# Down projection of the gated feed-forward by seven half-block products over pairs of inner tiles

## What is computed

```python
def conv_ffn(h, w_up, conv_w, conv_b, w_down):
    u = h @ w_up                       # 1024 -> 2 * 2816
    u = depthwise_conv(u, conv_w, width=3) + conv_b
    g, val = jnp.split(u, 2, axis=-1)
    return (jax.nn.silu(g) * val) @ w_down     # 2816 -> 1024
x = x + conv_ffn(rmsnorm(x, ffn_norm_g[i]), ...)
```

## Time and profile before

| | us |
|---|---|
| median of three runs | 2869.74 |
| lowest, highest | 2862.95, 2871.09 |
| profiled execution | 2867.41 |
| its span, first to last instruction | 2865.6 |
| PE busy in the span | 2743.9 |
| DVE, POOL, ACT busy | 1777.1, 1455.1, 1356.6 |

### The profile page before, as it was taken

How to read it: one execution, slowest core, us unless ns; L and a number is a source line. 1 busy time by engine, 2 the same in 40 slices (tenths; PEclk the granted TensorE clock), 3 DMA queues, 4 the chain that set the end, 5 groups by cost and what they waited for, 6 DMA issues and landing times. The chain is left out here.

```text
span 2865.6 us, 40261 instructions
## 1 busy us (share of the span) xinstructions
PE 2743.9 (96%) x13708; PEld 2308.6 (81%) x13708; DVE 1777.1 (62%) x2481; ACT 1356.6 (47%) x2102; POOL 1455.1 (51%) x1119
## 2 busy tenths in 40 slices
PE   8899999999989999999989999998898999999998
PEld 6788888877878888788878888887787788887886
DVE  6577777773654455555478887887527445545555
ACT  5577777763444444311256665665414444443212
POOL 2355555442587777543553333332226877774443
PEclk9999999999999999999999999999899999999999
DMA  3000000003122122522020010000320212225221
GB/s 137 23 11 10 7 7 10 15 1 149 57 89 88 67 87 88 198 99 106 15 112 23 32 35 24 30 26 13 151 105 30 103 73 88 88 72 221 88 88 59
DMA packets 54395, 195.37 MB, mean 68 GB/s; under 512 B 6544, under 2 KB 9872, under 8 KB 53776
## 3 DMA queue, kind: packets, MB, share of 16 engines
q1 hardware_dynamic: 54288, 193.95, 18.6%
HBM read 148.84 MB, written 45.09 MB: 68 GB/s over the span
## 5 line engine op out<-in xcount | busy, mean ns | idle before, releaser
L1209 PE MATMUL ffn_ps<-ffn_b_hi,weights_hi 128*128 128x512 f32 x704 | 278.6, 396 | 19.1 <-POOL weights_lo L720 10.2
L1210 PE MATMUL ffn_ps<-ffn_b_lo,weights_hi 128*128 128x512 f32 x704 | 276.6, 393 | 0.0
L1211 PE MATMUL ffn_ps<-ffn_b_hi,weights_lo 128*128 128x512 f32 x704 | 276.6, 393 | 0.0
L360 POOL TENSOR_TENSOR weights_lo<-weights_raw,weights_hi 128x1024 fp32r<-128x1024 f32 (+2 forms) x65 | 127.0, 1960 | 215.6 <-ACT weights_hi L355 215.6
L1100 POOL TENSOR_TENSOR ffn_y_lo<-ffn_y_raw,ffn_y_hi 128x1024 fp32r<-128x1024 f32 x44 | 109.0, 2498 | 231.1 <-ACT ffn_y_hi L1030 231.1
L720 POOL TENSOR_TENSOR up_local_lo<-up_sums,up_local_hi 128x512 fp32r<-128x512 f32 x126 | 171.4, 1363 | 96.8 <-ACT up_local_hi L715 96.8
L2301 ACT ACTIVATE dif_p<-dif_s,dif_neg_max 128x1024 f32<-128x1024 f32 x128 | 142.2, 1114 | 124.5 <-DVE dif_neg_max L2488 116.5
L1209 PE MATMUL ffn_ps<-ffn_b_hi,up_local_hi 128*128 128x512 f32 x504 | 196.3, 390 | 0.0
L1210 PE MATMUL ffn_ps<-ffn_b_lo,up_local_hi 128*128 128x512 f32 x504 | 196.1, 389 | 0.0
L1211 PE MATMUL ffn_ps<-ffn_b_hi,up_local_lo 128*128 128x512 f32 x504 | 196.1, 389 | 0.0
L1030 ACT ACTIVATE ffn_y_hi<-ffn_y_raw 128x1024 fp32r<-128x1024 f32 x44 | 44.2, 1051 | 315.0 <-PE ffn_ps L1211 315.0
(11 more groups left out here) (353 smaller groups left out, 8530.3 us busy)
## 6 DMA issues: line engine op xcount, KB each, us to landing
weights_raw<-in_up SPq DMA_DIRECT2D x44, 512.0 KB, 3.8
up_raw<-in_up SPq DMA_DIRECT2D x44, 512.0 KB, 4.1
ffn_products<-ffn_conv SPq DMA_DIRECT2D x44, 512.0 KB, 2.7
ffn_y_raw<-ffn_products SPq DMA_DIRECT2D x44, 512.0 KB, 4.1
ffn_down_raw<-in_down SPq DMA_DIRECT2D x24, 512.0 KB, 6.3
weights_raw<-in_diff_qkv SPq DMA_DIRECT2D x23, 512.0 KB, 3.6
weights_raw<-in_down SPq DMA_DIRECT2D x20, 512.0 KB, 5.9
x_spill<-x_in SPq DMA_DIRECT2D x16, 512.0 KB, 3.9
```

Source lines behind the costliest of these rows:

```text
L360: pool.tensor_tensor(w.lo[:], w.raw[:], w.hi[:].bitcast(F32), ALU.subtract).then_inc(w.lo_done, 1)
L1209: pe.matmul(out, hi, x_hi, start=start, stop=False, skip_group_check=True)
L1210: pe.matmul(out, hi, x_lo, start=False, stop=False, skip_group_check=True)
L1211: return pe.matmul(out, lo, x_hi, start=False, stop=stop, skip_group_check=True)
```

## The change

The down projection takes the same seven products as the up projection, over *pairs of inner tiles*. The weights of a pair (2 tiles x 8 output tiles) are split in four half blocks: A11 and A21 are the even tile's output tiles 0 to 3 and 4 to 7, A12 and A22 the odd tile's. The pair of y tiles is split in B11, B12 (even tile, left and right positions) and B21, B22 (odd tile). Sums of weights: S1 = A21 + A22, S2 = S1 - A11, S3 = A11 - A21, S4 = A12 - S2. Of y: T1 = B12 - B11, T2 = B22 - T1, T3 = B22 - B12, T4 = B21 - T2.

- **In the up projection** DVE makes T1 behind the gated product of an even tile and T2, T3, T4 behind that of an odd one (`finish_y`). SP stores B11 and T1, or B21, B22, T2, T3 and T4, each of 128 x 512, in place of one 128 x 1024 tile. ScalarE's centre tap of the value waits for those stores.
- **Groups** (`SUPER`): six; the first has one pair, the others two. A group has seven steps (`DOWN_A`, 42 in all). A step is one product: 4 output tiles x 1 or 2 pairs x 3 passes = 12 or 24 matmuls into 4 banks.
- **Order of the queues**: SP's `fetch(g)` loads y block n when step n of the group before is over, or its low part is done (n = 0, 1). The odd weights follow behind step 2. POOL makes the four sums and all low parts of weights in one fixed order. ScalarE's `high` copies a step's weights and then its y block, step by step. DVE makes the low parts of y, four steps ahead (`low_y(step + 4)`, then `add_product(step)`).
- **Additions**: steps 0, 1 of a group go to a buffer `common`, step 3 to `fifth`, the others straight to a quarter of `x_out`. In the last group DVE adds `common` and `fifth` to the quarters (16 additions) before the last three steps' own. Step 2 accumulates on step 0's banks and step 6 on step 5's, so TensorE's step 6 waits until DVE has read step 5's banks (`use = step - 1`); the others wait for the step two or three before.
- The order of the final squares and the place of `sq` follow.

```diff
+DOWN_A = ("A11", "S2", "A12", "S1", "S4", "S3", "A22")
+DOWN_SUMS = ("S1", "S2", "S4", "S3")
+SUPER = [(0, 1)] + [(2 * g - 1, 2) for g in range(1, 6)]
+STEPS = 7 * len(SUPER)
...
+            def fetch(g):
+                for n in range(2):
+                    sp.wait_ge(y_lo_done, 7 * g - 7 + n + 1)
+                    load_y(g, n)
+                sp.wait_ge(a_summed, 4 * g)
+                sp.wait_ge(a_lo_done, 7 * g - 6)
+                load_a(g, 0)
+                multiplied(sp, 7 * g - 5)
+                load_y(g, 2)
+                sp.wait_ge(a_lo_done, 7 * g)
+                load_a(g, 1)
+                for n in range(3, 7):
+                    multiplied(sp, 7 * g - 7 + n)
+                    load_y(g, n)
...
+            def high(g, n):
...
+                multiplied(act, step - 7)
+                if name in DOWN_SUMS:
+                    act.wait_ge(a_summed, 4 * g + DOWN_SUMS.index(name) + 1)
+                else:
+                    act.wait_ge(even_loaded if name == "A11" else odd_loaded, 32 * g + 16)
+                act.activation(down.a_hi[name][:, 0:width], down.a_raw[name][:, 0:width], ACT.Copy).then_inc(a_hi_done, 1)
+                act.wait_ge(y_loaded[n], 16 * g + 16)
+                act.activation(down.b_hi[n][:, 0:width], down.b_raw[n][:, 0:width], ACT.Copy).then_inc(y_hi_done, 1)
...
+            def sum_a(g, name, first, second, op, loads, sums):
...
+                multiplied(pool, 7 * g - 7 + DOWN_A.index(name))
...
+            for g in range(len(SUPER)):
+                sum_a(g, "S1", "A21", "A22", ALU.add, (even_loaded, odd_loaded), 0)
+                sum_a(g, "S2", "S1", "A11", ALU.subtract, (), 1)
+                low_a(g, "A11")
+                sum_a(g, "S4", "A12", "S2", ALU.subtract, (), 2)
+                pool.wait_ge(a_summed, 4 * g + 3)
+                low_a(g, "S2")
+                low_a(g, "A12")
+                low_a(g, "S1")
+                sum_a(g, "S3", "A11", "A21", ALU.subtract, (), 0)
+                low_a(g, "S4")
+                low_a(g, "S3")
+                low_a(g, "A22")
...
+            low_y(0)
+            low_y(1)
             finish(PAIRS - 1, 1)
...
+            add_product(0)
+            finish_y(PAIRS - 1, False)
+            low_y(2)
+            low_y(3)
+            low_y(4)
+            for step in range(1, LAST_COMMON + 1):
+                low_y(step + 4)
+                add_product(step)
...
+            add_common(6)
+            add_common(4)
+            add_product(STEPS - 3)
+            add_common(5)
+            add_product(STEPS - 2)
+            add_product(STEPS - 1)
...
-                        for z in range(2):
-                            mm = passes(bank(DOWN_BANKS[n % NACC]), down_hi[s][z][:, m, :], down_lo[s][z][:, m, :],
-                                        y_hi[s][:, z, cols], y_lo[s][:, z, cols], z == 0, z == 1)
-                        mm.then_inc(acc_ready, 1)
...
+                more = n in (2, 6)
+                use = step - {0: 3, 6: 1}.get(n, 2)
+                for i in range(4):
...
+                        pe.wait_ge(acc_added, added(use, i))
+                    for j in range(width):
+                        mm = passes(bank(DOWN_BANKS[4 * second + i]), down.a_hi[name][:, j, i, :],
+                                    down.a_lo[name][:, j, i, :], down.b_hi[n][:, j, :], down.b_lo[n][:, j, :],
+                                    j == 0 and not more, j == width - 1)
+                    mm.then_inc(acc_ready, 1)
```

More of the change, by code:

```diff
@@ L1040, in _ @@
             act.wait_ge(c21_done, PAIRS - 1)
[L1041 removed]
+            act.wait_ge(y_done, PAIRS - 1)
+            act.wait_ge(y_stored, stored(PAIRS - 1, False))
             centre(1, PAIRS - 1, 1)
[L1044 to L1054 removed]
+            for step in range(2, STEPS):
+                high(step // 7, step % 7)
             if ahead:
@@ L1109, in _ @@
-            groups(pool, step)
+            def sum_a(g, name, first, second, op, loads, sums):
+                width, raw_a = SUPER[g][1], down.a_raw
+                for done in loads:
+                    pool.wait_ge(done, 32 * g + 16 * width - (16 if g else 0))
+                need(pool, a_summed, 4 * g + sums)
+                multiplied(pool, 7 * g - 7 + DOWN_A.index(name))
+                pool.tensor_tensor(raw_a[name][:, 0:width], raw_a[first][:, 0:width], raw_a[second][:, 0:width],
+                                   op).then_inc(a_summed, 1)
@@ new lines, in shared, with add_common @@
+            def shared(n, i):
+                return added(LAST_COMMON, 3) + {6: 4, 4: 8, 5: 16}[n] + i + 1
+            def add_common(n):
+                for i in range(4):
+                    if n != 6:
+                        dve.wait_ge(acc_added, added(LAST_COMMON, 3) + i + 1)
+                    dve.tensor_tensor(x_part(n, i), x_part(n, i), (down.common if n == 6 else down.fifth)[:, i, :],
+                                      ALU.add).then_inc(acc_added, 1)
+            low_y(0)
+            low_y(1)
@@ new lines, in _ @@
+            finish(PAIRS - 1, 1)
+            add_product(0)
[6 more added lines that the diff above has]
+                add_product(step)
+            for i in range(4):
+                dve.wait_ge(acc_added, added(LAST_COMMON, i))
+                dve.tensor_tensor(down.fifth[:, i, :], down.fifth[:, i, :], down.common[:, i, :],
+                                  ALU.add).then_inc(acc_added, 1)
@@ new lines, in _ @@
+            multiply_down(0)
+            fourth(PAIRS - 1)
+            for step in range(1, STEPS):
+                multiply_down(step)
+            parts = ((out_norm.acc, 1, 0, out_norm.sq_added, 12), (out_norm.acc, 0, 0, out_norm.sq_added, 15),
+                     (sq[:, 1, :], 0, HALF, out_norm.sq_ready, 16))
+            for i, (squares, half, place, ready, count) in enumerate(parts):
+                pe.wait_ge(ready, count)
+                for t in range(4 * half, 4 * half + 4):
+                    mm = pe.matmul(out_norm.psum_sum[:, t:t + 1], squares[:, place + t * P:place + (t + 1) * P],
+                                   ones[:, 0:1], start=(i == 0 and t == 4), stop=(i == 2 and t == 3),
+                                   skip_group_check=True)
@@ L1304 @@
+            mm.then_inc(out_norm.sq_summed, 1)
 class Latent:
```

299 lines of the change are left out of this document (180 added, 119 removed).

## The result

The changed kernel took **2951.95 us** (median of four runs, 2947.85 to 2963.81) against 2867.74 us for the kernel before: ratio 1.0302, 95% interval 1.0266 to 1.0337, 3.0% slower. I had forecast 2923 us and a range up to 2946: the sign was right, the size too small by 29 us, and the time lies above the range. The profiled execution took 2963.81 us, with a span of 2961.5; it is the longest of the four, so sums made from its trace are up to 12 us larger than the medians say.

The account below looks back on a forecast made before the run. TensorE's instruction count was taken as the bound. Per layer 212.2 + 27.2 + 20.9 + 3.6 + 6.0 = 269.9 us, + 2.6 behind; both layers add 53.4 to 2867.4, median 2.3 above: 2923 us, range 2885 to 2946.

Parts of the forecast that it names:

- Removed work: Down projection: 924 matmuls a layer remain, 132 fewer, saving 29.9 us a layer, 59.8 us for both, all on the path.
- I take nothing: Up projection: DVE's added subtractions, 0.69 us each, delay block sums by 2.1 us in odd cycles but cost TensorE 0 us.
- gaps in the loop of the up projection: Sign in the up projection's loop: gaps there would show that its three subtractions were misjudged; it should stay 100% busy.
- The fallback of 20 us: Up projection: if the cover is gone, 1 us in 20 cycles is 20 us, half of it kept in the upper end.
- The low clock: Down projection: six new stalls a layer of over 3.5 us, each followed by 1.0 us lost at low clock: 6 us.
- The change of group: Down projection, groups 1 to 4: TensorE's seventh step waits for DVE's additions, 5.2 us each, 20.9 us a layer.
- a split port: Alternative to DVE and POOL taking turns: both run on at a slower rate, a layer's stretch some 10 us shorter.
- The first group: Start of the down projection, one pair with short steps: waits of 1.15, 3.5, 8.4, 2.5 and 11.6, 27.2 us a layer.
- The end: End of the down projection: DVE's shared additions, 0.68 us each, make the last step start 3.6 us late.
- waits feed each other: Rival, both layers: transfers at 6.3 us and more, low clock after each stall; +76 us, 2946; chance 0.17.

## Why the prediction was too low, point by point

- **Removed work.** Right: 924 matmuls a layer. Of the 616 first passes of both layers 528 stand in the rows of after, against the earlier trace rows:

```profile
L1372 PE MATMUL ffn_ps<-ffn_y_hi,ffn_hi_S x352: 389/389/796, 1209.7 to 2923.5; 128*128 128x512 f32 x176
...
L1372 PE MATMUL ffn_ps<-ffn_y_hi,ffn_hi_A x176: 387/389/767, 1202.5 to 2936.6; 128*128 128x512 f32 x176
```

- **The step that failed: "I take nothing" for the up projection.** It measured 15.7 and 15.6 us a layer. I had read from the earlier trace rows that a DVE instruction with both operands in SBUF waits for a POOL instruction to end, and even listed the product at 1174.87 with its 1.78 us, but priced three differences at 0.69 each, from a row whose second operand lies in PSUM. Beside POOL two of them took 1.56 and 1.78 us and the product ahead of them 2.02, the sums come 4.8 us later instead of 2.1, and the 1.21 us of slack in the earlier trace rows and the cycle behind it are used up. The sign that I had named for this, gaps in the loop of the up projection, came. The fallback of 20 us stood in the text for the case that the cover is gone; 31.3 us came in the two layers. I had also written that half of the 20 is kept in the upper end, but the upper end of 2946 is the rival's sum without it. With those 10 us the range would have reached 2956 and held the result, by an allowance and not by the mechanism.
- **The low clock: 6.0 us a layer forecast, 17.7 and 15.3 measured** (what the starts of matmuls without a wait lie further apart than 0.2267 us). I counted six stalls a layer of over 3.5 us at 1 us each; my own list had eight of 3.5 us and more, and ten in all. The trace of after has ten stalls a layer, and shorter ones pulled the clock down too. After 2.75 us idle in layer 0:

```profile
1331.21 0.47 PE L1372 MATMUL ffn_ps<-ffn_y_hi,ffn_hi_A 128*128 128x512 f32 x1 [2.75 <-DVE x_first L1331]
...
1332.67 0.59 PE L1372 MATMUL ffn_ps<-ffn_y_hi,ffn_hi_A 128*128 128x512 f32 x1
1333.06 0.63 PE L1373 MATMUL ffn_ps<-ffn_y_lo,ffn_hi_A 128*128 128x512 f32 x1
...
1336.04 0.44 PE L1374 MATMUL ffn_ps<-ffn_y_hi,ffn_lo_A 128*128 128x512 f32 x1
```

  Eight matmuls 0.43 us apart instead of 0.23. Layer 0's down projection has 81 such matmuls, layer 1's 70; before, seven (I had read eight) and none.
- **The change of group: mechanism right, size too large.** Forecast 4 x 5.2 us; measured 2.65, 2.75, 3.91, 2.83 and 3.33, 2.92, 3.20, 3.09. The rows of DVE and POOL at the second of them, whose group starts at 1295.66:

```profile
1318.62 2.39 POOL L1176 TENSOR_TENSOR ffn_raw_S<-ffn_a_raw 128x1024 f32<-128x1024 f32 x1 [9.86 <-DMA ffn_a_raw<-in_down]
```

```profile
1325.62 1.32 DVE L1306 TENSOR_TENSOR ffn_y_lo<-weights_raw,ffn_y_hi 128x1024 fp32r<-128x1024 f32 x1 [7.32 <-ACT ffn_y_hi L1117]
1326.86 2.47 DVE L1331 TENSOR_TENSOR x_first<-x_first,ffn_ps 128x512 f32<-128x512 f32 x4
1329.25 1.21 DVE L1306 TENSOR_TENSOR ffn_y_lo<-ffn_y_raw,weights_hi 128x1024 fp32r<-128x1024 f32 x1
1330.39 2.47 DVE L1331 TENSOR_TENSOR x_first<-x_first,ffn_ps 128x512 f32<-128x512 f32 x4
```

  POOL's S1 starts 23.0 us into the group (forecast 22.7), the first low part ends at 31.3 (31.2). The second low part was free to go at once, 1.21 us; I had it wait for POOL's sum S4, 3.5 us. Here DVE came first and POOL's next instruction had to wait (3.43 us for 2.4). Which of the two gets its turn first I had taken against DVE. The 10 us that I gave for a split port were not worked out from rows, and no run shows them.
- **The first group: 27.2 us forecast, 23.9 and 25.3 measured.** Its five stalls in layer 0 were 2.74, 3.30, 5.84, 4.06 and 7.91 us, against 1.15, 3.5, 8.4, 2.5 and 11.6.
- **The end: 3.6 us forecast, 12.2 and 5.7 measured.** The same omission as in the up projection. The shared additions have both operands in SBUF, and in layer 0 POOL prepares the next stage's weights and sums squares beside them:

```profile
1449.77 6.89 DVE L1358 TENSOR_TENSOR ffn_fifth<-ffn_fifth,ffn_common 128x512 f32<-128x512 f32 x4
1456.59 4.68 DVE L1342 TENSOR_TENSOR x_first<-x_first,ffn_common 128x512 f32<-128x512 f32 x4
```

```profile
1448.18 5.22 POOL L360 TENSOR_TENSOR weights_lo<-weights_raw,weights_hi 128x1024 fp32r<-128x1024 f32 x2 [10.82 <-ACT weights_hi L355]
...
1454.57 4.95 POOL L1208 TENSOR_TENSOR ffn_sq<-ffn_sq 128x512 f32<-128x512 f32 x3
```

  In layer 1, with POOL idle, four of them take 2.49 us, and only the last four, beside the squares, more:

```profile
2916.53 2.49 DVE L1342 TENSOR_TENSOR x_second<-x_second,ffn_common 128x512 f32<-128x512 f32 x4
...
2923.74 5.55 DVE L1342 TENSOR_TENSOR x_second<-x_second,ffn_fifth 128x512 f32<-128x512 f32 x4
```

```profile
2923.52 2.95 POOL L1208 TENSOR_TENSOR ffn_sq<-ffn_sq 128x512 f32<-128x512 f32 x2
```

  I had 0.68 for one throughout, the price alone. The 3.1 us more of that last set cover what layer 1's wait has beyond the forecast (5.7 us for 3.6).

Together, from the last matmul of the up projection on, layer 0 took 279.9 us and layer 1 272.7, against 269.9 forecast: the waits at the changes of group, 12.1 and 12.5 us for 20.9, hid part of the two terms that were too low. So the down projection was nearly right in sum by luck, since errors in both directions met there, and the up projection made the miss: 31.3 of the 43 us between the forecast and the profiled execution. The rival "waits feed each other", at 2946, was the nearest in time, but its price for the changes of group (26 us a layer) did not occur.

## What to carry to other kernels

When a trace has shown that two engines take turns, apply it to every instruction of that kind that the change adds, in every stage, before deciding that slack covers it; look for the form of the instruction (here, both operands in SBUF) and not for the place where it was first seen. In a queue in which additions free another engine's banks, put them ahead of whatever prepares operands several steps away: one exchanged pair of calls gave 34 us. And a removal on TensorE that splits its work into shorter steps with more side work can be paid at the edges, as here in the first group and behind the last step, where no steady state hides it; count the stalls and the clock behind each.

## What the runs showed of the hardware that I had not expected

- A DVE instruction of 512 columns with two SBUF operands took 1766 ns on average beside POOL (T1, L1266), and the same place filled with one that reads a single SBUF operand 686 ns. The gated product, which kept two operands, averaged 1.44 to 1.45 us in that kernel and 1.90 to 2.01 in the changed one: taking turns also delays the neighbours.
- In after the granted clock fell behind idle times of 2.65 to 3.3 us in eight of eleven cases, in two of them only 1.3 to 1.5 us after TensorE had started again, and then 5 to 14 matmuls came 0.43 us apart. With the longer stalls that was 15 to 18 us over a layer's down projection, about a quarter of all that was lost there.
